# The low parts of the mixing stages' weight chunks, moved from POOL to VectorE

## What is computed

```python
# a layer of the first block
h = rms_norm(x, norm_mix[l])
(m_qk, m_v, m_o, m_i, m_f, r_x, r_g, a_q, a_k, a_v, a_qi, a_ki, a_w, gates) = jnp.split(h @ w_in[l], split_at, axis=-1)
...
merged = (g_a * (y_a @ w_branch[l, 0]) + g_b * (y_b @ w_branch[l, 1]) + g_c * (y_c @ w_branch[l, 2]))
x = x + merged @ w_out[l]
...
x = x + (jax.nn.gelu(ff_g) * ff_u) @ ffn_down[l]
# the second block
proj = u @ w_in[l]
...
h = h + jnp.concatenate([y_ssd, y_sc], axis=-1) @ w_out[l]
h = h + hier_moe(u2, ...)
```

## Time and profile before

| | us |
|---|---|
| runs, median (lowest to highest) | 1795.41 (1789.62 to 1798.51) |
| the profiled execution | 1790.27 |
| its span in the trace | 1788.5 |
| busy: TensorE | 1632.9 |
| VectorE | 1277.1 |
| ScalarE | 948.4 |
| POOL | 716.1 |

### The profile page before, as it was taken

How to read it: one execution, slowest core, us unless ns; L and a number is a source line. 1 busy time by engine, 2 the same in 40 slices (tenths; PEclk the granted TensorE clock), 3 DMA queues, 4 the chain that set the end, 5 groups by cost and what they waited for, 6 DMA issues and landing times.

```text
span 1788.5 us, 28861 instructions
## 1 busy us (share of the span) xinstructions
PE 1632.9 (91%) x11632; PEld 1515.5 (85%) x11632; DVE 1277.1 (71%) x1456; ACT 948.4 (53%) x982; POOL 716.1 (40%) x236
## 2 busy tenths in 40 slices
PE   3889999799996979999899997799989899999997
PEld 3879989799996969989899997698889787787775
DVE  6598574565556498656365556855994799999997
ACT  5537454454444636555454444455543676767774
POOL 0544436200000444436400000243344399989884
PEclk9999999899998989999999999899999899999999
DMA  7434535555554434534645554334334499999993
GB/s 195 142 95 143 165 119 165 154 180 173 188 187 132 142 95 143 163 119 155 182 146 188 170 187 160 93 120 140 120 126 150 171 344 349 352 339 354 350 352 124
DMA packets 227949, 329.57 MB, mean 184 GB/s; under 512 B 26112, under 2 KB 184704, under 8 KB 227840
## 3 DMA queue, kind: packets, MB, share of 16 engines
q1 hardware_dynamic: 227840, 328.07, 55.8%
HBM read 327.00 MB, written 1.05 MB: 183 GB/s over the span
## 4 chain that ended last, share of the span: by engine, by line
PE 51%; issue 17%; DVE 16%; POOL 13%; ACT 2%; DMA 1%; POOLq 0%; SPq 0%; DVEq 0%; ACTq 0%
PE bank L2006 16%; PE bank L2007 15%; PE bank L2008 15%; POOL w_lo L645 11%; DVE w_lo L1836 5%; DVE w_lo_m L1836 1%; POOL work L661 1%; PE bank L2357 1%; POOL work L669 1%; DMA w_raw<-in_w_in 1%; PE bank L2463 1%; DVE nf L1807 1%; DVE work L1746 1%; DVE work L1222 1%; DVE work L1211 0%
## 5 line engine op out<-in xcount | busy, mean ns | idle before, releaser
L2006 PE MATMUL bank<-act_h,w_hi 128*128 128x256 f32 (+1 forms) x2176 | 627.4, 288 | 41.5 <-DVE act_l L1227 18.6
L2007 PE MATMUL bank<-act_l,w_hi 128*128 128x256 f32 (+1 forms) x2176 | 617.6, 284 | 0.0
L2008 PE MATMUL bank<-act_h,w_lo 128*128 128x256 f32 (+1 forms) x2176 | 616.7, 283 | 0.0
L645 POOL TENSOR_TENSOR w_lo<-w_raw,w_hi 128x2048 fp32r<-128x2048 f32 x71 | 332.3, 4682 | 412.7 <-ACT w_hi L721 242.2
L2006 PEld LDWEIGHTS bank<-act_h,w_hi 128*128 128x128 f32 x2176 | 416.2, 191 | 52.4 <-DVE act_l L1227 21.5
L2007 PEld LDWEIGHTS bank<-act_l,w_hi 128*128 128x128 f32 x2176 | 416.6, 191 | 0.5
L2008 PEld LDWEIGHTS bank<-act_h,w_lo 128*128 128x128 f32 x2176 | 415.6, 191 | 0.0
L1204 DVE TENSOR_TENSOR w_lo<-w_raw,w_hi 128x2048 fp32r<-128x2048 f32 x106 | 247.0, 2331 | 145.5 <-ACT w_hi L721 145.0
L721 ACT CAST w_hi<-w_raw 128x2048 fp32r<-128x2048 f32 x158 | 301.3, 1907 | 78.2 <-PE bank L2008 69.4
L2006 PE MATMUL bank<-y_h,w_hi 128*128 128x256 f32 x704 | 200.6, 285 | 5.2 <-DVE y_l L1552 2.9
L2007 PE MATMUL bank<-y_l,w_hi 128*128 128x256 f32 x704 | 198.1, 281 | 0.0
(11 more groups left out here) (439 smaller groups left out, 2885.8 us busy)
## 6 DMA issues: line engine op xcount, KB each, us to landing
w_raw<-in_w_in SPq DMA_DIRECT2D x88, 1024.0 KB, 5.5
w_raw<-in_ffn_up SPq DMA_DIRECT2D x48, 1024.0 KB, 5.1
w_raw<-in_e_gate SPq DMA_DIRECT2D x26, 1024.0 KB, 6.3
w_raw<-in_ffn_down SPq DMA_DIRECT2D x24, 1024.0 KB, 4.9
w_raw<-in_e_up SPq DMA_DIRECT2D x23, 1024.0 KB, 5.8
w_raw<-in_e_down SPq DMA_DIRECT2D x23, 1024.0 KB, 5.8
w_raw<-in_w_out SPq DMA_DIRECT2D x16, 1024.0 KB, 5.4
w_raw<-in_w_branch SPq DMA_DIRECT2D x12, 1024.0 KB, 5.0
```

The costliest lines, as they stand in the source:

```text
L645: nc.gpsimd.tensor_tensor(w_lo[c % RING][:], w_raw[c % RING][:], w_hi[c % RING][:].bitcast(F32), ALU.subtract).then_inc(sem[f"lo_ready{c % ...
L2006: mm(out, a_hi, b_hi, start=first, stop=False, skip_group_check=True)
L2007: mm(out, a_hi, b_lo, start=False, stop=False, skip_group_check=True)
L2008: return mm(out, a_lo, b_hi, start=False, stop=last, skip_group_check=True)
```

## The change

`pool_splits` and its uses go. VectorE makes the low part of chunk c+3 in every step of the mixing stages, at the place in its step where it made every third before. POOL's loops lose line 645 and keep everything else.

```diff
-def pool_splits(c, end):
-
-    return RING <= c < end and c % RING != 0
...
# POOL, layer(L), in the loop over c
-                    if pool_splits(c + RING, MIX):
-                        split(L, c + RING)
...
# POOL, second block
-            for c in range(MIX_2 - 1):
-                if pool_splits(c + RING, MIX_2):
-                    split(DEPTH, c + RING)
...
# VectorE, layer(L)
                     if c == MERGE:
 
                         side(L, c)
-                        if not pool_splits(c + RING, MIX):
-                            split(L, c + RING)
+                        split(L, c + RING)
                     elif c < MIX - 1:
-                        if not pool_splits(c + RING, MIX):
-                            split(L, c + RING)
+                        split(L, c + RING)
                         side(L, c)
...
# VectorE, second block
                 if c + RING < MIX_2:
-                    if not pool_splits(c + RING, MIX_2):
-                        split_2(c + RING)
+                    split_2(c + RING)
```

## The result

The changed kernel takes **1753.47 us** as a median (1751.38 to 1754.81), the kernel before 1793.24 beside it: a ratio of 0.976, interval 0.974 to 0.979. The profiled execution took 1751.38 us. All traces are compared by the moment at which TensorE starts its k-th matmul, which is the same matmul in every kernel here; "ahead by 5 us at 300" means that. All executions count in the medians; one, of the run for places 2 and 3, took 3372 us, and without it that run's median would be 1783.6 in place of 1784.7.

A forecast was written before the change was run, and what follows sets the result against it. Only time TensorE loses (91% busy) can be won: 7.0 + 4.0 - 1.7 + 6.2 = 15.5 us off the profiled 1790.3 gives 1774.8, plus 5.1 to the median, 1780 us; own range 1769 to 1790, tested range 1764 to 1797.

The forecast's parts named there:

- places 2 and 3: Step 26 and chunk 35 of each layer: TensorE's waits behind stretched lines shrink, 7.0 us won in two layers, bounds 0 and 12.
- place 1: Steps 5 to 14 of each layer, VectorE nearly full: vanished stretches are given back to added low parts, 0 won.
- place 4: Second block, chunk 4: the wait for line 1663 shrinks as line 1198's stretch goes, 4.0 us won, bounds 3 and 6.
- place 6: Second block, 1290 to 1357 us, VectorE full: waits go but 2.7 us at step 24; 6.2 won, bounds 2 and 8.
- place 5: Second block, steps 5 to 18: added low parts delay transposes and a head's weights, -1.7 us, bounds -5 and 0.
- loads that don't slip: Loads on SP's queue wait for the low parts, which end at most 0.3 us later than POOL's, mostly 2 earlier.
- the waits for line 1243: Evacuation of chunks 12 and 14: these waits replace shrinking ones for lines 1305 and 1321; over 20 us means place 1 misjudged.
- the wait for line 822: Step 26 of a layer, TensorE waiting for a square: from 2.6 us to under 2, and the clock stays up behind it.
- the four lines named: VectorE's lines 1321, 1486, 1445 and 1198: no duration over 2 us in the changed kernel's profile.
- Rival (b): The low part in front of side work eats the gains except at second block's chunk 4: 0 to 8 us, 1791; chance 0.21.
- Rival (c): Slower: VectorE bounds places 1 and 6 because less of the stretches returns than they hold; 20 us, 1815; chance 0.11.
- rival (a): VectorE has room everywhere, every wait hanging on a stretch vanishes, with some 12 us of half clock: 57 less, 1738; chance 0.08.

The follow-up runs named there:

- the run for places 2 and 3: Against the kernel before, only the low parts of chunks 19 to 41 of each layer that POOL made are moved to VectorE; 1784.73 us, ratio 0.994.

## Why the prediction was wrong

The forecast was 26.5 us too slow, and the step that failed most is the zero of place 1. By the table 9.8 of them arose at place 1, 5.5 at place 4, 3.2 at place 6, 2.7 at places 2 and 3, 0.9 at place 5, 1.3 elsewhere, and 3.0 in going from one execution to the median.

**What held.** The mechanism (a VectorE instruction lasts until POOL's is done), the places, POOL's 332 us, loads that don't slip (ScalarE waits for those of `in_w_in` 8.9 us before and 9.3 after), places 2 and 3 within their bounds (9.0 alone for 7.0), the waits for line 1243 that come in place of others (10.0 us, at most 20 were allowed for), the wait for line 822 (0.8 us, under 2 forecast), no stretch left on the four lines named. VectorE's busy time rose by 41.5, not 55: the stretches were counted too small by 14 us. Rival (b) falls with the gains at places 2, 3 and 6. Rival (c) falls too: it needed less than 10.6 us of stretches to return in place 1, and 14.6 did. The cases were drawn too far apart; the time lies between the forecast and rival (a), 15 us from the latter, to which a chance of 0.08 was given.

**Place 1 (0; measured 9.8, alone 11.2).** Two steps failed here. The first is the sum of 13.0 us of stretches, in which "0.8 in small ones" stood for 4.0: line 1484 at 2.33 us where it takes 1.21, two executions of line 1348 with 1.6 too much, and line 1369 with 1.3.

```profile
L1369 DVE TENSOR_SCALAR work<-work x4: 1456/1690/1752, 139.8 to 721.9; 128x256 f32<-128x256 f32 x2, 128x128 f32<-128x128 f32 x2
```
```profile
L1359 DVE TENSOR_SCALAR work<-work x4: 226/260/294, 137.6 to 710.2; 128x256 f32<-128x256 f32 x2, 128x128 f32<-128x128 f32 x2
```

Lines 1484 and 1369 are never short in the trace of before, so comparing an instruction with its own line's shortest finds nothing there. Only about half of the 4.0 lay beside a low part. Line 1484 (1.1 too much) and one execution of line 1348 (1.0) stood beside POOL's products with the cosines, which POOL keeps; VectorE's line, then POOL's:

```profile
104.56 2.33 DVE L1484 TENSOR_TENSOR work<-work 128x1024 f32<-128x1024 f32 x1
```
```profile
104.23 1.58 POOL L661 TENSOR_TENSOR work<-work,cos_t 128x512 f32<-128x512 f32 x1 [2.43 <-ACT work L765]
```

That these two came free is luck of the new timing, and the same products took 1.6 back at line 1286. The net in front of chunk 12's evacuation was then 3.1 us and not 1.5; in the first layer's trace VectorE starts it 3.5 us earlier than before (138.31 us for 141.84). The second step that failed is that TensorE stands at chunk 17 where it stood. It did give back a half: 10.0 us ahead at 140 us of the first layer, it was 4.8 ahead from chunk 17 on. But the two new waits, 3.4 and 1.6, are less than the waits that went, and less half clock follows them.

**Place 4 (4.0; measured 9.5, alone 8.6).** The stretch of line 1759 (2.6) was missing, and "the half clock gets a little shorter" was 2.3 us. **Place 6 (6.2; 9.4):** the 2.7 us left at step 24 weren't there. **Place 5 (-1.7; -0.8)** was too dear.

**The clock.** The prediction took 1.7 us of clock in each layer, at place 2 (1.6 there, by the run), and nearly nothing elsewhere. 9.4 us came. Behind the wait of 6.9 us at chunk 4 the clock is 0.50, and with the wait the half clock went; at place 1 the mean clock rose too. Rival (a) had it, at 12.

**From one execution to the median.** 5.1 us were added because the median of before stood that far above its profiled execution; after it is 2.1, and three of the 26.5 us are this. The second pattern of steps 5 to 14, which the change removes, is the likeliest source, but no trace of a slower execution of the kernel before shows it.

## What to carry to other kernels

When an engine seems slow in some instructions, compare their durations with the same form anywhere, or with the cost per column, not with the best of the same line. Where VectorE and POOL work side by side on operands in SBUF, try two things: cut POOL's instruction until it is about as short as VectorE's beside it (better here where VectorE was full), or give the whole job to VectorE (better here in the second block and the experts). And look for half clock behind a wait of TensorE before pricing it. In sum it was 9.4 us beside 29.6 of waits here, and 33 beside 67 with the low parts made twice; behind the waits of place 6, up to 3.3 us each, there was none.

## What the runs showed of the hardware

- In the traces with pieces the two engines alternate instruction by instruction. A scan of 0.66 us takes 1.11 to 1.17 beside pieces of 256 columns, 2.8 beside pieces of 1024, 5.0 beside 2048. A piece of 256 columns costs POOL 0.74 us where an eighth of the whole is 0.58.
- An instruction with one tensor as input can be held too. Line 1369 is one: it takes 1.46 to 1.75 us and ends with POOL's low part, where after the change it takes 0.226 us for 128 columns and 0.294 for 256. Line 1396, on 8 columns, took 3.37 beside a low part and 0.17 without. From 128 to 256 columns line 1369 grows by 0.53 ns a column, line 1348 with two inputs (0.352 and 0.485 us) by 1.0. The Trainium skill (SBUF — State Buffer, Who interferes with whom) counts `tensor_scalar` among the operations that can run in a faster mode and then contend with GpSimd; by that rule, the trace agrees. The prediction had told only of instructions with two SBUF tensors, and its reciprocal does keep its time.
- VectorE instructions that read PSUM and one SBUF tensor (line 1243) keep their time beside POOL's low part: 0.47 to 0.48 us in all 72 executions, some twenty of them beside one.
- The Trainium skill (Perfetto Trace Analysis, Optimizing Scalar/DVE Operations) says that offloading from a saturated VectorE to GpSimd may make sense, but might not help because of the shared port. Its warning held with instructions of 2048 columns and in the experts, where less VectorE work on paper was more VectorE time, 2.80 us against 2.29. With POOL's instruction cut in eight, the offloading did pay in the layers.
- The kernel with these collisions spread more than the one without: 1788.6 to 1804.4 us in 19 executions, 1751.4 to 1754.8 in 4. The unequal counts make this less sure than it looks.

Not tried: POOL kept busy in the kernel after with instructions that don't read SBUF. It stays open whether a POOL instruction that only writes would hold VectorE as well.
